# First stage of a two-group encoder layer: conditioning weights outside the weight ring, and the first block's input projection in plain float32

## The reference, cut to what matters

```
mod = jax.nn.silu(c) @ w_ada + b_ada            # w_ada: 1024 x 6144
sh1, sc1, gt1, sh2, sc2, gt2 = split(mod, 6)
h = rmsnorm(x, g_pre_mix) * (1 + sc1) + sh1
proj = h @ w_in                                 # 1024 x 2176
mix = concat(pool(xa), conformer_conv(xb), short_conv(xc)) @ w_out
x = x + gt1 * rmsnorm(mix, g_post_mix)
h = rmsnorm(x, g_pre_ffn) * (1 + sc2) + sh2
x = x + gt2 * rmsnorm((silu(h @ w_gate) * (h @ w_up)) @ w_down, g_post_ffn)
```

## Time and profile before

| | |
|---|---|
| median of 3 runs | 2328.3 us |
| the profiled execution | 2328.53 us, of it span 2326.7 us |
| PE busy | 97% of the span, 12444 matmul instructions |
| PE weight load busy | 90% |
| DVE busy | 58% |
| ACT busy | 44% |
| DMA | 361.64 MB, mean 155 GB/s |
| mean granted TensorE clock | 0.987 of full |

### The profile page before, as it was taken

The page is one execution under the profiler, slowest core; times in us unless marked ns, Lnnn a source line. Parts: engine busy times, 40 slices in busy tenths (PEclk is TensorE's granted clock), DMA queues, the critical chain, the costliest instruction groups (busy, mean ns, idle before and its releaser), DMA issues.

```text
span 2326.7 us, 30257 instructions
## 1 busy us (share of the span) xinstructions
PE 2265.7 (97%) x12444; PEld 2084.1 (90%) x12444; DVE 1351.2 (58%) x1937; ACT 1027.3 (44%) x1432; POOL 40.7 (2%) x82
## 2 busy tenths in 40 slices
PE   7879999999999999999999999999999999999998
PEld 3658899997999898999999899989889997899987
DVE  3767886489553477844357774436784534443343
ACT  4445456546263544445353435344443424433332
POOL 0000000000000000000000000000000000000000
PEclk8989999999999999999999999999999999999999
DMA  7754464354533353453344354335335433544332
GB/s 296 277 212 172 151 211 156 121 193 159 199 125 127 118 181 127 154 173 126 127 151 156 119 181 151 126 123 181 127 125 174 128 127 109 181 148 161 127 126 91
DMA packets 101743, 361.64 MB, mean 155 GB/s; under 512 B 12259, under 2 KB 14435, under 8 KB 101604
## 3 DMA queue, kind: packets, MB, share of 16 engines
q1 hardware_dynamic: 101606, 359.71, 44.1%
HBM read 340.73 MB, written 18.93 MB: 155 GB/s over the span
## 4 chain that ended last, share of the span: by engine, by line
PE 89%; DVE 4%; issue 1%; ACT 1%; DMA 1%; POOL 0%; SPq 0%; POOLq 0%; ACTq 0%; DVEq 0%
PE ps L520 88%; DVE wlo L1147 1%; DVE pr L1280 1%; PE ps L572 1%; DMA raw<-in_w_gu 0%; DVE g_lo L1196 0%; PE ps L540 0%; DMA raw<-in_w_mix 0%; DVE h_lo L1189 0%; ACT whi L787 0%; DVE xr L1220 0%; ACT junk L829 0%; ACT junk L806 0%; DVE xt L1210 0%; DVE y_pr L1439 0%
## 5 line engine op out<-in xcount | busy, mean ns | idle before, releaser
L1147 DVE TENSOR_TENSOR wlo<-raw,whi 128x1024 fp32r<-128x1024 f32 x546 | 664.2, 1221 | 543.9 <-ACT whi L787 542.8
L520 PE MATMUL ps<-h_hi,whi 128*128 128x384 f32 (+1 forms) x2928 | 960.7, 328 | 11.1 <-DVE wlo L1147 9.4
L520 PE MATMUL ps<-h_lo,whi 128*128 128x384 f32 (+1 forms) x2928 | 955.2, 326 | 0.0
L520 PE MATMUL ps<-h_hi,wlo 128*128 128x384 f32 (+1 forms) x2928 | 955.1, 326 | 0.0
L787 ACT ACTIVATE whi<-raw 128x1024 fp32r<-128x1024 f32 x546 | 575.5, 1057 | 791.2 <-DMA raw<-in_w_gu 530.2
L520 PEld LDWEIGHTS ps<-h_hi,whi 128*128 128x128 f32 x2928 | 553.9, 189 | 19.0 <-issue 14.3
L520 PEld LDWEIGHTS ps<-h_lo,whi 128*128 128x128 f32 x2928 | 553.9, 189 | 2.3 <-issue 0.5
L520 PEld LDWEIGHTS ps<-h_hi,wlo 128*128 128x128 f32 x2928 | 553.7, 189 | 0.0
L520 PE MATMUL ps<-whi,g_hi 128*128 128x512 f32 x748 | 236.1, 397 | 7.0 <-DVE g_lo L1196 6.0
L520 PE MATMUL ps<-whi,g_lo 128*128 128x512 f32 x748 | 231.7, 391 | 0.0
L520 PE MATMUL ps<-wlo,g_hi 128*128 128x512 f32 x748 | 231.7, 391 | 0.0
(11 more groups left out here) (119 smaller groups left out, 1173.8 us busy)
## 6 DMA issues: line engine op xcount, KB each, us to landing
raw<-in_w_gu SPq DMA_DIRECT2D x264, 512.0 KB, 3.2
raw<-in_w_mix SPq DMA_DIRECT2D x150, 512.0 KB, 3.2
raw<-in_w_dn SPq DMA_DIRECT2D x132, 512.0 KB, 3.2
raw<-in_w_ada SPq DMA_DIRECT2D x38, 512.0 KB, 5.2
xt<-in_x_all SPq DMA_DIRECT2D x17, 512.0 KB, 5.9
xr<-in_x_all SPq DMA_DIRECT2D x17, 512.0 KB, 5.9
xr<-x_all SPq DMA_DIRECT2D x17, 512.0 KB, 5.9
x_all<-xr SPq DMA_DIRECT2D x5, 1536.0 KB, 7.4
```

The costliest lines, as they stand in the source:

```text
L520: return nc.tensor.matmul(out, lhsT, rhs, start=start, stop=stop, skip_group_check=True)
L1147: tt(wlo[:, s, :], raw[:, s, :], whi[:, s, :].bitcast(F32), ALU.subtract).then_inc(w_lo, 1)
```

## The change

- STREAM holds no conditioning unit any more. Fours 4 to 11 are numbered f = 0 to 7 in the order of their use (FOURS = 6, 7, 8, 9, 4, 5, 10, 11) and loaded by `load_four` into tiles that are free in the first stage: even f into xr and u, odd f into gate1, gate2, gate1_first and gate2_first. Each f has a semaphore; `four_used` counts the fours used. Four f waits for four_used f - 1.
- The 17 units of block 0's projection are neither split nor multiplied three times: `project_first` multiplies the raw weights by an unsplit input h_first in plain float32, eight matmuls a unit (16 instructions). `modulate` and `modulate_samples` write h_first (a slot for each k) for the first norm; `h_split` and `h_rest` of that norm are gone. Splitting begins with unit 17 (WHOLE), at j = 13 of block 0.
- The gpost rows and the residual input of block 0 are loaded after `load("out", 0, 1)` and a wait for all eight fours, since their tiles hold fours before.
- VectorE hands out 5 steps where it handed out 4 (and 2 for each unit of a four), and waits for four_used 7 before it writes u.

```
+FOURS = [6, 7, 8, 9, 4, 5, 10, 11]
+FOUR_IN = {5: 0, 8: 1, 11: 2, 14: 3}
+FOUR_EARLY = {1: 6, 3: 7}
+STREAM = [("in", 0, j_) for j_ in range(NIN)]
+STREAM += [("in", 1, j_) for j_ in range(EARLY)]
...
+WHOLE = NIN
...
-IN_FIRST, IN_FOUR, IN_BETWEEN, IN_EARLY, IN_OUT = 4, 2, 3, 6, 2
+IN_FIRST, IN_BETWEEN, IN_EARLY, IN_OUT = 5, 3, 6, 2
...
+            h_first = sb("h_first", [P, KD, NT[0] * P], scope=under, align=OPERAND)
...
+        def four_place(f, i):
+            if f % 2:
+                return (gate1, gate2, gate1_first, gate2_first)[i][:, :]
+            return xr[:, i, :] if i < TB else u[:, :, :].rearrange("p j n -> p (j n)")[:, 0:D]
...
+            def load_four(f):
+                if f >= 2:
+                    sp.wait_ge(four_used, f - 1)
+                for i in range(STRIPS):
+                    sp.dma_start(four_place(f, i), w_ada[STRIPS * FOURS[f] + i]).then_inc(four_landed[f], 16)
...
             for j in range(NIN):
                 load("in", 0, j)
                 if j == RING - 1:
+                    load_four(0)
                     sp.wait_ge(t_full, KD)
                     load_x(1)
+                if j == 7:
+                    load_four(1)
...
-                if j == 14:
-                    for i, dst in enumerate((gate1, gate2)):
-                        sp.dma_start(dst[:, :], gpost[i:i + 1, :].to_broadcast([P, D])).then_inc(gpost_landed, 16)
+                if j == 12:
+                    load_four(2)
+                if j == 15:
+                    load_four(3)
             for j in range(EARLY):
                 load("in", 1, j)
                 if j == 1:
-                    sp.wait_ge(cols_full, 2)
-                    sp.dma_start(mod[BIAS:MOD_K, 0:1, :], b_ada[:, 5:6]).then_inc(bias_landed[2], 16)
+                    load_four(4)
+                if j == 4:
+                    load_four(5)
+            load_four(6)
+            sp.wait_ge(cols_full, 2)
+            sp.dma_start(mod[BIAS:MOD_K, 0:1, :], b_ada[:, 5:6]).then_inc(bias_landed[2], 16)
+            load_four(7)
...
                 for k in range(NMIX):
                     load("out", c, k)
+                    if c == 0 and k == 1:
+                        sp.wait_ge(four_used, len(FOURS))
+                        for i, dst in enumerate((gate1, gate2)):
+                            sp.dma_start(dst[:, :], gpost[i:i + 1, :].to_broadcast([P, D])).then_inc(gpost_landed, 16)
+                        load_res(x_v, 0)
...
+            def project_first(j):
+                n, w = UNIT["in", 0, j], NT[0] * P
+                if j >= 2:
+                    pe.wait_ge(evac_done, evac_count(0, j - 2))
+                else:
+                    pe.wait_ge(t_read, KD - 1 + j)
+                pe.wait_ge(w_landed[n % RING], landed(n))
+                for k in range(KD):
+                    if j == 0:
+                        pe.wait_ge(t_read, k + 1)
+                        pe.wait_ge(sample_mod, k + 1)
+                    last = mm(ps[:, j % 2, 0:w], chan(raw[:, n % RING, :])[:, k, :], h_first[:, k, :], k == 0, k == KD - 1)
+                last.then_inc(w_used, 1)
...
-            for n in range(LEAD):
-                high(n)
             for k in range(KD):
                 modulate(0, k)
-                h_split(0, k)
-                if k >= KD - 2:
-                    high(LEAD + k - (KD - 2))
             for j in range(NIN):
-                if j >= RING - LEAD:
-                    ahead("in", 0, j)
+                ahead("in", 0, j)
...
-                if j in FOUR_EARLY:
-                    for n in four(FOUR_EARLY[j]):
-                        ahead("ada", n)
-            ada_out(FOUR_EARLY[3] // 2)
+            ada_out(FOURS[7] // 2)
...
-            for n in range(3):
-                low(n)
             columns(0, 6)
-            modulate_samples(0, 0)
             for k in range(KD):
-                if k + 1 < KD:
-                    modulate_samples(0, k + 1)
-                h_rest(0, k)
-                if k == 5:
-                    low(3)
-            for n in range(LEAD, RING):
-                low(n)
+                modulate_samples(0, k)
```

More of the change, by code:

```diff
@@ L210, in build @@
             h_pre = sb("h_pre", [P, 2 * TB, D], scope=under, align=OPERAND)
+        with ExitStack() as under:
+            h_first = sb("h_first", [P, KD, NT[0] * P], scope=under, align=OPERAND)
         h_hi = sb("h_hi", [P, KD, N], F32R, align=OPERAND)
@@ L271, in build @@
         pre_used = sem("pre_used")
+        four_landed = [sem(f"four_landed{i}") for i in range(len(FOURS))]
+        four_used = sem("four_used")
         w_landed = [sem(f"w_landed{i}") for i in range(RING)]
@@ L533, in ada_units @@
                         if at < PRE:
-                            src, there, count, used = pre(at), pre_landed[at], 16, pre_used
-                        else:
[L536 to L539, removed]
+                            src = pre(at)
+                            if h == 0:
+                                pe.wait_ge(pre_landed[at], 16)
+                        else:
+                            src = four_place(FOURS.index(q), i)
                         last = nc.tensor.matmul(ps[strip:strip + C_PAD, 2 + 2 * ADA_PAIR[g] + h, :], c_s[:, k0 + i, :],
@@ L542, in ada_units @@
                                                 stop=k0 + STRIPS == KD, tile_position=(0, strip), skip_group_check=True)
-                        if h:
-                            last.then_inc(used, 1)
+                        if h and at < PRE:
+                            last.then_inc(pre_used, 1)
+                if q >= PRE // STRIPS:
+                    last.then_inc(four_used, 1)
             def ada_columns(bank):
@@ L790, in ahead @@
                 n = UNIT[key] + LEAD
-                if n < TOTAL and STREAM[n][0] != "ada":
+                if WHOLE <= n < TOTAL:
                     high(n)
@@ L963, in _ @@
                         x_normalise(1, t)
-                if j in FOUR_IN:
-                    for n in four(FOUR_IN[j]):
-                        ahead("ada", n)
-                    if FOUR_IN[j] % 2:
-                        ada_out(FOUR_IN[j] // 2)
+                if FOUR_IN.get(j, 0) % 2:
+                    ada_out(FOURS[FOUR_IN[j]] // 2)
             for k in range(KD):
-                ahead("ada", STRIPS * FOUR_BETWEEN[0] + k)
                 modulate(1, k)
                 h_split(1, k)
-            ada_out(FOUR_BETWEEN[1] // 2)
+            ada_out(FOURS[5] // 2)
             for j in range(EARLY - 2):
@@ L1399, in mixing @@
                     dve.wait_ge(z_ready, NCONV * (b + 1))
+                    if first:
+                        dve.wait_ge(four_used, len(FOURS) - 1)
                     for j in range(NCONV):
@@ L1473, in _ @@
             for j in range(NIN):
+                ahead("in", 0, j)
                 if j >= RING - LEAD:
-                    ahead("in", 0, j)
                     advance(mixer, IN_FIRST)
                 if j in FOUR_IN:
-                    for n in four(FOUR_IN[j]):
-                        ahead("ada", n)
-                        advance(mixer, IN_FOUR)
+                    advance(mixer, IN_FIRST)
             for k in range(KD):
-                ahead("ada", STRIPS * FOUR_BETWEEN[0] + k)
                 advance(mixer, IN_BETWEEN)
@@ L1489, in _ @@
                 advance(mixer, IN_EARLY)
[L1490 to L1493, removed]
             finish(mixer)
```

52 lines of the change are left out of this document (20 added, 32 removed).

## The result

The changed kernel takes 2314.3 us (median of 5 runs, 2312.4 to 2319.4) where the kernel before takes 2328.3 us: a ratio of 0.9937, 95% interval 0.9921 to 0.9954, 14.0 us less. A second set of the same two kernels gave 0.9942 (0.9930 to 0.9955). Forecast were 2312.5 us, and 2306 to 2319.

The account below looks back on a forecast made before the run. PE, busy 97% of the span, was taken as the bound, with gains only in the first 170 us. Terms sum to -15.8 us from 2328.5: 2312.7 for the profiled execution, 2312.5 as median, range 2306 to 2319.

Parts of the forecast that it names:

- Parts 1 and 2: Block 0's projection: plain float32 loses 11.9 us, stalls and clock give back 13.4; 70.9 instead of 72.5 us.
- rival 1: Plain float32 dearer, 0.24 us an instruction instead of 0.224: +4.4 us, 2317 us; chance 0.12.
- The four-pass rule: Block 0: true float32 takes four array passes; at 0.12 us each, 0.48 us a matmul, 65.3 us for the block.
- Part 3: Start, before block 0's projection: fewer low parts on DVE and a shorter modulation chain gain 1.3 us, at least 0.
- Part 4: Between the projections of blocks 0 and 1: gain 2.8 us, 0 at worst, 4.6 at best.
- Part 5: Early projections of block 1: 1.0 us low-part wait goes, idle 1.2 instead of 9.2 us, statistics at full clock gain 2.0.
- Part 6: Ahead of the variance statistic: loads behind the new wait delay unit 25; stall 0.9 us, 2.5 by the longer landing.
- PE idle time after 150 us that was not there before: One of the signs that would show the prediction wrong.
- 4: Rival: weight loads of plain float32 do not hide in block 0, at most 52 us, 2364, slower than before; chance 0.05.
- 2: Rival: DVE takes ACT's place ahead of the statistics and the clock falls: 4 + 2 us, 2318.5; chance 0.08.
- 3: Rival: memory rate, not the ring, causes block 0's stalls of about 12 us, which stay: 2325 us; chance 0.05.
- part 1: Block 0: plain float32 at 0.224 us an instruction takes 60.9 us where fp32r took 49.0, a loss of 11.9 us.

Follow-up runs that it names:

- e2: Changed kernel, but block 0's projection again split into three fp32r matmuls, fours still outside the ring: 0.9917 of the kernel before.
- e4: Kernel before, with one line moved: ACT's last conditioning copy goes ahead of the four high parts that stood before it: 0.9971.
- e1: Changed kernel, but gpost and residual input asked for behind unit (out, 0, 3) instead of (out, 0, 1): 0.9910 of the kernel before.
- c1: The changed kernel run once more, unaltered, as control: 0.9942 of the kernel before.
- e3: Kernel before, with only the plain float32 projection of block 0 and its unsplit input, fours still in the ring: 1.0000.
- e6: e2 with e1's edit, and VectorE's mixing steps dealt 4 instead of 5 in block 0, 12 instead of 6 beside early projections: 0.9899 of the kernel before.
- e7: e1, with block 1's squares and their sum ahead of the two high and low parts of the same step: 0.9917 of the kernel before.
- e8: e6 with e7's edit (squares and sum ahead of the splits of the same step): 2302.7 us, 0.9885 of the kernel before.

## Why the prediction was right, point by point

**Parts 1 and 2.** A plain float32 instruction costs (5.56 - 0.38) / 24 = 0.216 us in the long stream at 83.70, not 0.224: 17 x 16 x 0.216 = 58.8 us, 2.1 us less than forecast and inside the bounds. The row of the right shape was the worse guide; the wide matmuls of the earlier trace rows gave 0.215. With fours and the slow start the forecast was 70.9 us for what took 70.5 to the first transpose. That the two agree within 0.4 us is in part luck: the matmuls took 2.1 us less, and most of it was lost again. The slow start is one place: 96 instructions up to the first four at 67.38 us took 23.7 us where 0.216 each make 20.7, so it cost 2.9 us and not 2.0. The gain is 2.8 us and not 1.6, because the kernel before, put at 72.5 us by its parts, takes 73.3 to the same place (44.32 to 117.59). The stalls went entirely, as the waits show. The price of 0.24 us an instruction in rival 1, made from the distance of fp32r matmuls, was too high. The four-pass rule of the Trainium skill (FP8 and Floating Point Precision, TensorE Precision Notes) agrees with the trace if a pass is priced by its columns (four times 256 columns at 2.4 GHz are 0.43 us, measured 2 x 0.216).

**Part 3.** The chain saved what was forecast, 31.86 to 43.72 against 31.13 to 44.32 are 1.3 us; the start is only 0.6 us earlier because the columns began 0.7 us later in this execution.

**Part 4.** 15.1 us, forecast 15.0. DVE was not late with plain float32; it was in e2, where the split stayed.

**Part 5.** The idle time is 1.19 us, forecast 1.2, and the statistics ran at full clock. e4 shows the cause by itself. It also shows what the prediction did not ask: with the fours still in the ring 4.1 us come back one step later, so the 8 us needed both the order and the free ring.

**Part 6 is the term that was mis-sized.** Its mechanism was right: unit 25 behind 2 MB of gpost and residual input, PE waiting ahead of the variance statistic. I took the shorter landing (5.4 us from the earlier trace rows, stall 0.9 us). Unit 25 landed 7.6 us behind its issue, and the stall was 2.4 us, the longer end. The clock was left out: behind that wait the statistic ran at half of it and took 1.4 us more, 3.8 of the 3.9 us in the table. e1 takes the whole of it away. The prediction also named PE idle time after 150 us that was not there before as a sign of being wrong; this stall is one, and the sum itself had put it at 0.9 us, so that sign contradicted part 6.

**The sum.** 15.8 us were forecast, 13.3 are there at the second gate rows, and the medians have 14.0 and 13.1 (c1). Part 6 cost 3.0 us more than its term, and the start and block 0 together gained 0.5 us more than theirs; the 1.5 us that both executions lose in the feed-forward stand in no term. The range held, but the start of the kernel alone moved one execution against another by 1.35 us, so an agreement of 2 us is not finer than the measurement.

**Rivals.** 1 and 4 fell by 0.216 us an instruction. 2 did not occur: DVE ended its pooling copies at 150.0, and the statistics began at 151.29. 3 fell by the waits. What none of them said is that the float32 half was no help to the time: e3 gives 1.0000, e2 a gain at least as large as the change's. The sum of part 1 had the fact (11.9 us lost) but set it against stalls that the other half removes anyway.

## What to carry to other kernels

When a change has two halves that cure the same wait, price each without the other: here moving short-lived loads out of the ring of the main stream cured it, and the dearer matmuls cost the busiest engine 9.8 us to relieve one whose work could be dealt otherwise (e6). A wait labelled issue is worth reading in the queue of the engine that releases it; one copy moved ahead of units that had not landed gave 5.6 to 6.8 us. Where loads are put behind a new wait, count the bytes that now stand between the wait and the next load on the path, and allow for the clock: behind the stalls of 2.4 us (the changed kernel) and 2.7 us (c1) the statistic ran at half clock, 2.93 us instead of 1.50, while behind 2.3 us in e2 it took 1.56.

## What the runs showed of the hardware that was not expected

Executions of one kernel differ by up to 7 us (2312.4 to 2319.4), and part of it is the granted clock: 0.95 in one profile of the changed kernel and 1.00 in another over the 31 us behind the same wait, which lasted 2.58 us in the first and 1.49 in the second. Over the first 5.6 us of the feed-forward, by contrast, two executions of the changed kernel agree (0.50 and 0.50), and so do kernels that are alike up to there: e1 and e7 have 0.66 and 0.66, e6 and e8 0.77 and 0.76, the kernel before 0.78. Plain float32 on 256 columns streams at 0.216 us an instruction, 1.3% above its columns at 2.4 GHz (0.213), while fp32r needs 0.12 us for 0.107 us of columns, 12% above: three fp32r matmuls cost 0.36 us where one plain float32 matmul costs 0.43, not a third more but a fifth.
